# Two transformer blocks on one core: the rotary turns read PSUM and run inside the next projection, latents ahead of queries

## The reference

```python
# layer 0: eight heads of kind A, eight of kind B
h = x @ w_in
qa, ka = apply_rope(h[..., :o1]), apply_rope(h[..., o1:o2])      # 8 tiles of 128 features: "qkA"
cq  = rms_norm(h[..., o3:o4], q_norm, RMS_EPS)                   # 384 latents: "lat" 0 to 2
ckv = rms_norm(h[..., o4:o5], kv_norm, RMS_EPS)                  # 256 latents: "lat" 3 and 4
qb  = cq @ w_q_up      # its last 32 features per head are rotated: "qB"
k_pe = apply_rope(h[..., o5:])                                   # "kpe"
# layer 1: eight heads of kind C
h = x @ w_qkv
q, k = apply_rope(h[..., :C_QK]), apply_rope(h[..., C_QK:2 * C_QK])   # 16 tiles: "qkC"
a = softmax(q @ k.T * dh ** -0.5)
o = (a[0] - lam * a[1]) @ v

def apply_rope(x, cos, sin, rot):
    x1, x2, rest = x[..., :half], x[..., half:rot], x[..., rot:]
    return concatenate([x1 * c - x2 * s, x2 * c + x1 * s, rest], -1)
```

## Time and profile before

| | |
|---|---|
| median of 3 executions | 2569.52 us (2565.92 to 2574.81) |
| the profiled execution: its own time, its span | 2566.32 us, 2564.5 us |
| busy: PE, DVE, ACT, POOL | 96%, 46%, 27%, 75% of the span |
| mean granted clock of PE | 0.978 of full speed |
| projections and rotations qkA, latents, kpe | 37.9 to 119.9 us |
| heads A, mixer_b, heads B | 128.9 to 289.9 us |
| mixer_c ends, heads C begin | 921.2 us, 927.95 us |

### The profile page before, as it was taken

How to read it: one execution, slowest core, us unless ns; L and a number is a source line. 1 busy time by engine, 2 the same in 40 slices (tenths; PEclk the granted TensorE clock), 3 DMA queues, 4 the chain that set the end, 5 groups by cost and what they waited for, 6 DMA issues and landing times.

```text
span 2564.5 us, 32275 instructions
## 1 busy us (share of the span) xinstructions
PE 2449.4 (96%) x11118; PEld 1888.2 (74%) x11118; DVE 1187.4 (46%) x1587; ACT 701.3 (27%) x1266; POOL 1913.4 (75%) x1553
## 2 busy tenths in 40 slices
PE   7988989999999989899999999999999999999998
PEld 6745668888867843678888677857888878578886
DVE  7485473330261676663320475556332654563323
ACT  2264333330021147233320133145010231450101
POOL 8804379888877953678888789735999897359995
PEclk9999999999999999999999999999999999999999
DMA  4201012222222210122222222211222222112222
GB/s 172 90 1 42 34 70 103 98 95 94 99 74 99 91 41 1 66 74 98 98 98 98 75 106 97 82 50 50 99 97 100 88 102 74 50 50 99 91 99 88
DMA packets 57547, 207.11 MB, mean 81 GB/s; under 512 B 6512, under 2 KB 6896, under 8 KB 57200
## 3 DMA queue, kind: packets, MB, share of 16 engines
q1 hardware_dynamic: 55872, 199.87, 22.3%
q10 hardware_dynamic: 1584, 5.96, 0.6%
HBM read 203.71 MB, written 2.10 MB: 80 GB/s over the span
## 4 chain that ended last, share of the span: by engine, by line
PE 77%; DVE 9%; POOL 7%; issue 4%; ACT 2%; DMA 0%; POOLq 0%; DVEq 0%; ACTq 0%; SPq 0%
PE bank L717 21%; PE bank L719 21%; PE bank L718 21%; POOL w_hi L2473 4%; PE bank L809 3%; PE bank L764 3%; POOL w_lo L2476 3%; PE bank L837 2%; PE bank L858 2%; DVE branch_lo L1812 1%; PE bank L879 1%; DVE work L1852 1%; DVE moving_lo L1812 1%; ACT region L1682 0%; PE bank L1209 0%
## 5 line engine op out<-in xcount | busy, mean ns | idle before, releaser
L2473 POOL TENSOR_TENSOR w_hi<-ring,unit 128x512 fp32r<-128x512 f32 x750 | 840.8, 1121 | 510.1 <-PE bank L719 371.5
L2476 POOL TENSOR_TENSOR w_lo<-ring,w_hi 128x512 fp32r<-128x512 f32 x750 | 1031.1, 1375 | 58.8
L717 PE MATMUL bank<-moving_hi,w_hi 128*128 128x512 f32 x1962 | 774.5, 395 | 24.7 <-DVE moving_lo L2088 12.3
L718 PE MATMUL bank<-moving_lo,w_hi 128*128 128x512 f32 x1962 | 768.1, 391 | 0.0
L719 PE MATMUL bank<-moving_hi,w_lo 128*128 128x512 f32 x1962 | 767.9, 391 | 0.0
L717 PEld LDWEIGHTS bank<-moving_hi,w_hi 128*128 128x128 f32 x1962 | 370.9, 189 | 113.5 <-issue 23.6
L718 PEld LDWEIGHTS bank<-moving_lo,w_hi 128*128 128x128 f32 x1962 | 370.9, 189 | 78.7 <-issue 1.7
L719 PEld LDWEIGHTS bank<-moving_hi,w_lo 128*128 128x128 f32 x1962 | 370.5, 189 | 78.5
L2420 DVE TENSOR_TENSOR region<-region,bank 128x512 f32<-128x512 f32 x64 | 39.7, 682 | 278.3 <-PE bank L719 278.3
L809 PE MATMUL bank<-region 64*128 64x512 f32 (+3 forms) x448 | 130.3, 599 | 15.7 <-DVE region L1806 4.4
L717 PE MATMUL bank<-hid_hi,w_hi 128*128 (+1 forms) x352 | 137.7, 391 | 0.0
(11 more groups left out here) (292 smaller groups left out, 3533.9 us busy)
## 6 DMA issues: line engine op xcount, KB each, us to landing
ring<-in_weights SPq DMA_DIRECT2D x375, 512.0 KB, 3.2
x<-in_x_t ACTq DMA_DIRECT2D x4, 512.0 KB, 8.4
out<-region SPq DMA_DIRECT2D x8, 256.0 KB, 2.2
region<-in_tables ACTq DMA_DIRECT2D x1, 1312.0 KB, 6.0
region<-in_tables ACTq DMA_DIRECT2D x1, 1024.0 KB, 5.5
region<-in_p_t ACTq DMA_DIRECT2D x2, 512.0 KB, 4.9
region<-in_tables SPq DMA_DIRECT2D x1, 320.0 KB, 10.2
small_w<-in_small_w ACTq DMA_DIRECT2D x1, 320.0 KB, 5.9
```

Of the source, the lines that this page charges most:

```text
L717: pe.matmul(bank, lhs[0], rhs[0], start=start, stop=False, skip_group_check=True)
L718: pe.matmul(bank, lhs[0], rhs[1], start=False, stop=False, skip_group_check=True)
L2473: pool.tensor_tensor(w_parts[0][:, s, at], ring[:, s, at], unit[:, 0:1].broadcast_to([P, BLK // 2]), ALU.mult).then_inc(split_hi, 1)
L2476: pool.tensor_tensor(w_parts[1][:, s, at], ring[:, s, at], w_parts[0][:, s, at].bitcast(F32), ALU.subtract).then_inc(split_ready, 1)
```

## The change

- Weight order: lat and kpe come before qkA; kpe is the first rotation. The sums of squares stand behind the projection of qkA 0, and DVE inverts and scales the latents one step at a time between the rotations qkA (`latent_norms`) and no longer in heads A.
- `raw` makes no copy for the first block's rotations; `raw_upper` makes the upper part alone. `rope_first` forms the lower part and the cosine product straight from the projection's PSUM bank and then frees it (`rope_freed`). `rope_second` multiplies by the sine inside the turned bank and adds.
- `turn_pairs` of tile t-1 stands in the middle of the projection of tile t (`halfway`).
- The last rotations (qkA 7, qkC 15) stand behind the first scores of the heads; DVE does their second half behind the first maximum.
- `mixer_b`: both first halves ahead of both second halves.
- Heads C: `copy_turned` of three turns ago stands ahead of a turn's exponentials. Small instructions of one column ahead of heads A and C and at the end of heads C make ACT load the tables for Exp and Sqrt there.

```diff
     keys = []
-    keys += [("vA", i) for i in range(4)] + [("qkA", t) for t in range(8)]
-    keys += [("lat", t) for t in range(5)] + [("kpe", 0)]
+    keys += [("vA", i) for i in range(4)]
+    keys += [("lat", t) for t in range(5)] + [("kpe", 0)] + [("qkA", t) for t in range(8)]
     keys += [("qup", i) for i in range(3)] + [("kvk", 0), ("kvv", 0)]
...
-    jobs = [("qkA", t) for t in range(8)] + [("kpe",)] + [("qB", r) for r in range(2)]
+    jobs = [("kpe",)] + [("qkA", t) for t in range(8)] + [("qB", r) for r in range(2)]
...
-        rope_parts = parts("rope", 0, 2, S, base=prob_at)
+        rope_parts = parts("rope", 4, 2, S, base=prob_at)
...
-            def project(key, bank, rhs, ready=None):
+            def project(key, bank, rhs, ready=None, halfway=None):
...
                     if k == KD // 2:
                         mm.then_inc(half_done, 1)
+                        if halfway:
+                            halfway()
                         arrived(key, 1)
...
                 for u, i in turns[:AHEAD]:
                     scores(u, i, q, k, extra, causal)
+                    if last_rope and i == 0:
+                        turn_pairs(last_rope, perm_a, P)
+                        pe.wait_ge(rope_freed, ROPE_AT[last_rope] + 1)
+                if last_rope:
+                    pe.wait_ge(roped, ROPE_AT[last_rope] + 1)
                 for n, (u, i) in enumerate(turns):
                     if n + AHEAD < len(turns):
...
                 for u, i in turns[:ST - 1]:
                     scores(u, i, q, k, lambda u: [])
+                    if i == 0:
+                        turn_pairs(("qkC", 15), perm_a, P)
+                        pe.wait_ge(rope_freed, ROPE_AT[("qkC", 15)] + 1)
+                pe.wait_ge(roped, ROPE_AT[("qkC", 15)] + 1)
...
-                for t in range(8):
-
-                    if t < 4:
-                        pe.wait_ge(v_stored, T["v"][("A", t)])
-                    else:
-                        pe.wait_ge(rope_raw, ROPE_AT[("qkA", t - 4)] + 1)
-                    project(("qkA", t), psum[t % 4][:], moved)
-                    if t:
-                        turn_pairs(("qkA", t - 1), perm_a, P, qk_a[:, t - 1, :])
                 for n in range(5):
...
-                sum_squares(None, psum[6], 3, lambda n: lat_square[:, n, :], lambda n: ("lat", n))
-                sum_squares(None, psum[7], 2, lambda n: lat_square[:, 3 + n, :], lambda n: ("lat", 3 + n))
-                turn_pairs(("kpe",), perm_b, B_QK, kpe[0:B_QK, :])
+                for t in range(8):
+                    if t >= 4:
+                        pe.wait_ge(rope_freed, ROPE_AT[("qkA", t - 4)] + 1)
+                    elif t == 1:
+                        pe.wait_ge(rope_freed, ROPE_AT[("kpe",)] + 1)
+                    else:
+                        pe.wait_ge(lat_raw, 5 if t == 0 else t + 1)
+                    turn_last = (lambda: turn_pairs(("qkA", t - 1), perm_a, P)) if t else (
+                        lambda: turn_pairs(("kpe",), perm_b, B_QK))
+                    project(("qkA", t), psum[t % 4][:], moved, halfway=turn_last)
+                    if t == 0:
+                        sum_squares(None, psum[6], 3, lambda n: lat_square[:, n, :], lambda n: ("lat", n))
+                        sum_squares(None, psum[7], 2, lambda n: lat_square[:, 3 + n, :], lambda n: ("lat", 3 + n))
...
-                    pe.wait_ge(roped, ROPE_AT[("kpe",)] + 1)
+                    pe.wait_ge(roped, ROPE_AT[("qkA", 6)] + 1)
...
-                turn_pairs(("qkC", 15), perm_a, P, qk_c[:, 15, :])
+                        pe.wait_ge(rope_freed, ROPE_AT[("qkC", t - 4)] + 1)
+                    if t == 1:
+                        pe.wait_ge(v_stored, T["v"][("C", 7)])
+                    project(("qkC", t), psum[t % 4][:], moved,
+                            halfway=(lambda: turn_pairs(("qkC", t - 1), perm_a, P)) if t else None)
...
+            def raw_upper(job, src, scale=1.0):
+                g = ROPE_AT[job]
+                if g >= 2:
+                    act.wait_ge(rope_perm, g - 1)
+                act.activation(rope_parts[0][0:src.shape[0], g % 2, :], src, ACT.Copy, scale=scale).then_inc(rope_raw, 1)
...
+                act.activation(table_in[:, 0:1], col("eps_ln"), ACT.Exp)
                 for n, (u, i) in enumerate(turns):
                     t = TURN_AT[(u, i)]
                     act.wait_ge(turned, max(t - 2, first_c))
+                    if n >= 3:
+                        copy_turned(*turns[n - 3])
                     for c in range(2):
                         act.wait_ge(maxed, 2 * t + c + 1)
                         at = 2 * (t % 4) + c
                         act.activation(blend_slot(t, c), psum[2 * (t % 2) + c], ACT.Exp, bias=negmax[:, at:at + 1],
                                        accum_out=rowsum[:, at:at + 1]).then_inc(exped, 1)
-                    if n >= 3:
-                        copy_turned(*turns[n - 3])
                     if i == 3 and n > 2 * ST:
                         finish(units[n // ST - 2])
+                act.activation(table_in[:, 1:2], col("eps_ln"), ACT.Sqrt)
                 for at in turns[-3:]:
...
+            def rope_first(job, bank, tile, cos, scale=1.0):
+
+                g, rows = ROPE_AT[job], tile.shape[0]
+                hi, lo = (part[0:rows, g % 2, :] for part in rope_parts)
+                dve.wait_ge(rope_raw, g + 1)
+                dve.scalar_tensor_tensor(out=lo, in0=bank, scalar=scale, in1=hi.bitcast(F32), op0=ALU.mult,
+                                         op1=ALU.subtract).then_inc(rope_split, 1)
+                dve.scalar_tensor_tensor(out=tile, in0=bank, scalar=scale, in1=cos, op0=ALU.mult,
+                                         op1=ALU.mult).then_inc(rope_freed, 1)
+
+            def rope_second(job, tile, sin, outs=None):
+
+                g, rows = ROPE_AT[job], tile.shape[0]
+                bank = psum[4 + g % 2][0:rows, :]
+                dve.wait_ge(rope_perm, g + 1)
+                dve.tensor_tensor(bank, bank, sin, ALU.mult).then_inc(rope_sined, 1)
+                dve.wait_ge(rope_sined, g + 1)
+                dve.wait_ge(rope_freed, g + 1)
+                for out, at in outs or [(tile, slice(0, rows))]:
+                    ins = dve.tensor_tensor(out, bank[at], tile[at], ALU.add)
+                ins.then_inc(roped, 1)
...
+                rope_first(("kpe",), psum[1][0:B_QK, :], kpe[0:B_QK, :], cos_b[0:B_QK, :])
+                steps = latent_norms()
                 for t in range(8):
-                    rope(("qkA", t), qk_a[:, t, :], P, cos_a, sin_a)
-                rope(("kpe",), kpe[0:B_QK, :], B_QK, cos_b[0:B_QK, :], sin_b[0:B_QK, :])
+                    if t == 0:
+                        rope_second(("kpe",), kpe[0:B_QK, :], sin_b[0:B_QK, :])
+                    else:
+                        rope_second(("qkA", t - 1), qk_a[:, t - 1, :], sin_a)
+                        steps[t - 1]()
+                    rope_first(("qkA", t), psum[t % 4][:], qk_a[:, t, :], cos_a, HD ** -0.5 if t < 4 else 1.0)
+
             def mixer_b():
                 for r in range(2):
+                    rope_first(("qB", r), psum[r][:], q_rope[:, r, :], cos_b, B_QK ** -0.5)
+                for r in range(2):
 
...
+                steps = [lambda: rope_second(("qkA", 7), qk_a[:, 7, :], sin_a)]
...
-                    rope(("qkC", t), qk_c[:, t, :], P, cos_a, sin_a)
+                    if t:
+                        rope_second(("qkC", t - 1), qk_c[:, t - 1, :], sin_a)
+                    rope_first(("qkC", t), psum[t % 4][:], qk_c[:, t, :], cos_a, HD ** -0.5 if t < 8 else 1.0)
...
+                    if n == 0:
+                        rope_second(("qkC", 15), qk_c[:, 15, :], sin_a)
```

90 lines of the change are left out of this document (42 added, 48 removed).

## The result

Before 2569.6 us (2565.9 to 2574.8), changed 2534.9 (2534.4 to 2539.5), ratio 0.9867, 95% interval 0.9847 to 0.9888: 1.3% faster. The forecast was 2543.9 with a range of 2534 to 2556, so the median lies 0.9 us above the lower end of the range. The profiled executions have spans of 2564.5 and 2533.2 us, 31.3 apart, where the sum had 25.6. That is more than the 22 to 28 us to which the forecast gave its 0.62, and lies in the bracket of its rival "more than counted", 28 to 32, which had 0.10.

The account below looks back on a forecast made before the run. PE was taken as the bound, busy 2449 of 2564.5 us. Terms sum to 27.1 us, less 1.5 for clock: gain 25.6, span 2538.9, own time 2540.7; with 3.2 for the median, 2543.9 us, range 2534 to 2556.

Parts of the forecast that it names:

- more than counted: Rival, chance 0.10: clock holds in heads A and C, spreads after heads C start at full clock; gain 28 to 32 us.
- Steady blocks unchanged: Projection blocks: rotation in the middle of the next projection costs the same 5.92 us per block; gain and loss none.
- eaten: Rival, chance 0.05: late lower parts inside the projection blocks lose 21 of 27 us, no change to be seen, 2564.
- slower: Rival, chance 0.03: DVE bounds the projections, a rotation's four operations taking 7.0 us against 5.92; 2581.
- First scores A: Stage one to heads A: latent sums and kpe's turn move into the projections, so first scores come 4.3 us earlier.
- First turns of A: Start of heads A: fourth turn's maximum 11.6 us after the first scores instead of 14.9, gain 3.3 us.
- `mixer_b`: PE's gap at the second rotation's turn goes, 6.6 us, and kvk runs at full clock, 2.1 us.
- Junction to C: `mixer_c` to heads C: first scores no longer wait for the turns of qkC 14 and 15, gain 6.8 us.
- ramp: Heads C, first scores to first transposes: about 9.0 us instead of 9.5, table load done while ACT idles; gain 0.5 us.
- Copies: Heads C: copies ahead of the exponentials remove seven waits for copied transposes, 2.5 us; gain counted 2.2 us.
- Sqrt: End of heads C: loading the Sqrt table ahead takes its load from before the deviations, gain 1.3 us.
- Clock allowance: Heads A and C: scores and transposes at half clock would show once DVE is quicker; 1.5 us taken off the gain.

Follow-up runs that it names:

- the four later executions: The changed kernel measured again with no line different: 2538.8 us, ratio to before 0.9877.
- e7: Changed kernel with rotations reading SBUF copies again, ScalarE's second copy back, and the order kept: span 2553.5 us.
- e6: Changed kernel with the latents' seven norm steps put back between the first turns of heads A: span 2542.9 us.
- e3: Changed kernel with only the order of the two query rotations in mixer_b undone, still reading PSUM: span 2537.3 us.
- e4: Changed kernel with the last rotation of A's and C's projections put back ahead of the first scores: span 2541.9 us.
- e1: Changed kernel with the copies in heads C put back behind the two exponentials: span 2541.6 us.
- e8: Kernel before with only the copies ahead of the exponentials in heads C and the three tables loaded ahead: span 2562.8 us.
- e2: Changed kernel without the three small activations that load function tables ahead: span 2534.0 us.

## Why the prediction was right, and where its sizes were off

The mechanisms were right but for one: in `mixer_b` the order was not the means that the prediction took it for. What it named as signs of being right all came: no wait over 1 us between the first projections (38 us) and heads A, first scores at 124.15, blocks of 5.92, no gap and full clock in `mixer_b`, heads C at 903.86, no wait for copies. The size was less good. The 5.7 us between the forecast gain of 25.6 and the measured 31.3 are 1.5 of copies priced too low, 1.0 at the start and in the first turns of A, 1.5 of clock allowance, and 1.7 behind the spread, which is the luck of one execution's clock. That the first median lies inside the range, 0.9 us above its end, is narrow too; the four later executions have 2538.8.

- *Steady blocks unchanged*: right. A lower part from PSUM in 0.69 us, blocks of 5.92, no wait inside `mixer_c`. The rivals "eaten" and "slower" are out, the second even with both operands in SBUF (e7: 4.0 us of DVE per block, not 7.0).
- *First scores A*, 4.3: measured 4.78. The last block ended 0.45 us earlier than worked out.
- *First turns of A*, 3.3: measured 3.83. The fourth turn's maximum began 11.05 us behind the first scores, where 11.6 was worked out; e6 gives 5.8 for the norms alone, with the clock's fall in it and with the new second half of the rotation still ahead of them.
- *`mixer_b`*, 8.7: measured 8.66, of which e3 leaves 8.05 without the order. What decided is what I had only as a choice, additions at 0.70. At 5.5 us for four (e7), PE waits 5.54 us ahead of the value products, more than the 4.1 that I kept for the range. The order, which I described as the change's means, is worth 0.6 (e3).
- *Junction to C*, 6.8, and *ramp*, 0.5: measured 6.82 and 0.46. Of the 6.8, e4 gives 3.8 to the place of the last rotation; the other 3.0, the shorter way from the last projection to the turned tile, were not undone alone. The 0.46 holds 0.66 us of half clock, which the forecast counted elsewhere; at full clock the ramp is 8.36 (e6), 1.1 less than before. PE's two waits of 1.4 us in it were not named in the forecast; its sum of DVE's and ACT's pieces contained them.
- *Copies*, 2.2: mis-sized, 3.65 (e1 3.43, e8 3.80). The step was to price seven waits by their printed length; six turns were 0.6 longer each.
- *Sqrt*, 1.3: measured 1.37 (e2, e8). The load of Exp ahead of heads C, which the prediction counted into the ramp, is worth 0.85 (e2 against e6).
- *Clock allowance*, -1.5: too large. The clock stayed at 1.00 in A. It fell in the ramp of C and cost 0.66 us there, behind waits of 1.4 us; that speaks against the reason the prediction gave for "more than counted", gaps too short for a fall. Between first scores A and first scores B the kernel before had lost 8.5 us' worth of full clock, the changed one none. The prediction counted 2.1 of them, in `mixer_b`; the rest lay mostly where DVE set the pace.
- *Median 3.2 above the profiled execution*: did not carry over. The eight executions of the changed kernel lie in two clumps, four from 2534.4 to 2535.3 and four from 2538.5 to 2539.9. The profiled one is of the lower. The middle of all eight is 2536.9, which is 7 below the forecast.

One thing was not tested alone: the weight order, which moves the latents ahead of the queries. e6 undoes only the norms that it makes possible, and the 4.8 us at the first scores of A are the new order, the last rotation's place (4.0 in e4) and the operands (1.9 in e7) together; the last two overlap, since they add up to more than the whole.
